# A mixture-of-experts encoder step on one core: later hand-overs while experts are gathered

## The reference

```python
h = rmsnorm(x, norm1_w) * (1.0 + sc1) + sh1
z = h @ w_in + b_in
ya = rglru(...)                       # 4 blocks of 128 channels
yb = mlstm(...)                       # 4 heads; state C, n carried over the tokens
x = x + g1 * (concat([ya, yb]) @ w_out)
h2 = rmsnorm(x, norm2_w) * (1.0 + sc2) + sh2
# peer, for each token, 8 heads:
q = rms(h2 @ wq)                      # 256 per head
v1, i1 = top_k(q1 @ k1.T, 16); v2, i2 = top_k(q2 @ k2.T, 16)
sv, si = top_k(v1 + v2, 16)           # of 256 candidates
expert = i1[si // 16] * 128 + i2[si % 16]
act = gelu(u[expert] . h2)
out = sum over 128 experts of softmax(sv) * act * v[expert]
y = rmsnorm(x + g2 * out, final_norm_w)
```

## Time and profile before

| | |
|---|---|
| median of 3 runs | 3409.78 us (3409.64 to 3411.5) |
| the profiled execution: its own time | 3413.67 us |
| its span, in which all rows stand | 3411.9 us |
| mean granted PE clock | 0.674 of full |
| busy PE, DVE, ACT, POOL | 70%, 65%, 58%, 36% of the span |
| DMA read and written | 1182.83 MB and 9.25 MB |
| first gather issued at | 531.31 us |

### The profile page before, as it was taken

One profiled execution on the slowest core, in us unless ns is written; L12 is line 12 of the kernel. 1 busy time (PEld: TensorE's weight loads), 2 busy tenths in 40 slices (PEclk: granted clock), 3 DMA queues, 4 the chain that ended last, 5 costly groups with the idle time before them and its releaser, 6 DMA issues.

```text
span 3411.9 us, 45621 instructions
## 1 busy us (share of the span) xinstructions
PE 2374.3 (70%) x15134; PEld 1117.1 (33%) x15134; DVE 2217.8 (65%) x5518; ACT 1985.6 (58%) x6404; POOL 1237.9 (36%) x1118
## 2 busy tenths in 40 slices
PE   7999976777567766666666666666666666676554
PEld 5665453333223322332322232223222332232110
DVE  5677255654576767666666666667666666667655
ACT  3332144554576766666576666666666666666655
POOL 0000102222344444444344434444444444434332
PEclk9999987888666666566556656666666566655555
DMA  7231317777999999999999999999999999999998
GB/s 276 85 113 60 78 69 248 279 281 268 364 420 401 369 421 420 397 420 420 417 393 420 420 404 413 420 420 394 420 420 420 395 420 420 420 393 420 421 421 349
DMA packets 184160, 1195.09 MB, mean 350 GB/s; under 512 B 22122, under 2 KB 32906, under 8 KB 44530
## 3 DMA queue, kind: packets, MB, share of 16 engines
q0 software_dynamic: 154240, 1113.16, 80.6%
q1 hardware_dynamic: 29684, 79.02, 6.7%
HBM read 1182.83 MB, written 9.25 MB: 349 GB/s over the span
## 4 chain that ended last, share of the span: by engine, by line
PE 36%; DMA 31%; ACT 18%; DVE 8%; issue 3%; POOL 3%; SPq 0%; DVEq 0%; POOLq 0%; ACTq 0%
DMA r_w<-in_peer_uv,gidx 11%; DMA r_vo<-in_peer_uv,gidx 10%; DMA r_yT<-in_peer_uv,gidx 9%; PE ps L953 9%; PE ps L1013 7%; PE ps L770 6%; PE ps L913 4%; PE ps L1002 4%; ACT mixc L1349 3%; PE ps L827 3%; ACT mixc L1348 3%; ACT r_qk L1353 3%; ACT L1348 2%; ACT mixc L1346 2%; DVE r_vo L1937 2%
## 5 line engine op out<-in xcount | busy, mean ns | idle before, releaser
L674 POOL DMA_INDIRECT r_vo<-in_peer_uv,gidx x272 | 321.2, 1181 | 509.1 <-PE ps L1013 465.1
L1013 PE MATMUL ps<-r_vo,r_qk 128*32 128x256 f32 x2176 | 264.9, 575 | 343.4 <-ACT r_qk L1353 342.8
L1345 ACT ACTIVATE mixc<-mixc 128x1 f32<-128x1 f32 x1056 | 208.8, 198 | 497.4 <-DVE r_yT L1937 153.4
L1013 PE MATMUL ps<-r_qk 128*32 128x256 f32 x2176 | 264.7, 575 | 284.4 <-ACT r_qk L1353 284.4
L674 POOL DMA_INDIRECT r_w<-in_peer_uv,gidx x241 | 286.8, 1190 | 458.2 <-PE ps L1013 442.0
L1349 ACT ACTIVATE mixc<-mixc 128x1 f32<-128x1 f32 x1056 | 409.1, 387 | 35.2
L674 POOL DMA_INDIRECT r_yT<-in_peer_uv,gidx x271 | 281.9, 1040 | 400.9 <-PE ps L1013 371.9
L674 POOL DMA_INDIRECT r_qk<-in_peer_uv,gidx x272 | 314.5, 1156 | 304.6 <-PE ps L1013 279.4
L1348 ACT ACTIVATE mixc<-mixc 128x1 f32<-128x1 f32 x1056 | 395.9, 375 | 1.0
L1013 PE MATMUL ps<-r_yT,r_qk 128*32 128x256 f32 x2168 | 254.4, 562 | 159.4 <-ACT r_qk L1353 145.6
L1353 ACT ACTIVATE r_qk<-prm,mixc 128x32 f32<-128x32 f32 x1056 | 340.0, 322 | 34.3
(11 more groups left out here) (331 smaller groups left out, 4380.0 us busy)
## 6 DMA issues: line engine op xcount, KB each, us to landing
r_w<-in_ada_w SPq DMA_DIRECT2D x18, 1024.0 KB, 5.4
r_w<-in_w_lin SPq DMA_DIRECT2D x16, 512.0 KB, 7.1
r_w<-in_peer_wq SPq DMA_DIRECT2D x6, 1024.0 KB, 21.0
r_hT<-in_peer_wq SPq DMA_DIRECT2D x6, 1024.0 KB, 13.2
r_vo<-in_peer_uv,gidx POOLq DMA_INDIRECT x272, 13.9
r_qk<-in_peer_uv,gidx POOLq DMA_INDIRECT x272, 14.9
r_yT<-in_peer_uv,gidx POOLq DMA_INDIRECT x271, 15.0
r_vo<-in_x_prompt SPq DMA_DIRECT2D x8, 512.0 KB, 7.1
```

The lines of the kernel that those rows point to most:

```text
L674: pool.indirect_dma_start(ring[i], None, table, bass.IndirectOffsetOnAxis(gidx_t[:, t % 2, h, c:c + 1], 0)).then_inc(e_ld[i], 16)
L1013: mm = nc.tensor.matmul(ps[c * DEC:(c + 1) * DEC, q // 2, (q % 2) * QC:(q % 2 + 1) * QC], diag[:, s % 4, :], row[:, D + c * QC:D + (c + 1) ...
L1345: wch.mark(nc.scalar.activation(sq[:, i:i + 1], d, ACT.Square, scale=GELU_C ** 0.5 / TANH_K))
```

## The change

Five things are changed; no computation is added or left out.

1. The chunk loop: from step 4 on `gated` and `turn_y` handle chunk i - 2 (`turned_y` i - 3), with `gated` ahead of `mixed_heads`. The work for tile 0 (x1 norm, scaling, turn, query, scores, route of head 0) moves one step earlier, and the norm of route 1 is moved ahead of the slot loop on ACT.
2. Hand-overs in the slot loop: a projection's pieces on PE go from offsets 0, 1, 5, 6 to 0, 2, 7, 9, its evictions on DVE from 3 and 8 to 7 and 14, `scaled` from 11 to 18; in a route the ACT part of the query goes from offset 0 to 2, the scores from 2 to 4, the first DVE step from 5 to 8, `copy_places` from 17 to 23 (12 to 18 in the short form).
3. The tables: projections every 14 slots in place of 10 (the last tile at slot 104 in place of 74), so `JOIN` goes from 92 to 108; routes 4 to 15 every 13 or 14 slots in place of gaps from 8 to 23.
4. Tile 1 takes its heads 4 to 7 first (`number`, `tile_head`, `SETS`), and POOL and ACT wait for one head's indices and gates at a time, not for those of a whole set.
5. The start of a tile: `final_sum` from slot 1 to 3, with what follows it; the sample head's query goes with the seventh head of a tile in place of the head S_AT = 5.

```diff
-JOIN = 92
+JOIN = 108
-SETS = [((0,), (1,), (2, 3), (4, 5), (6, 7)), ((0, 1), (2, 3), (4, 5, 6, 7))] + [
+SETS = [((0,), (1,), (2, 3), (4, 5), (6, 7)), ((4, 5), (6, 7), (0, 1, 2, 3))] + [
     ((0, 1, 2, 3), (4, 5, 6, 7))] * (NT - 3) + [((0,), (1,))]
-FAST = (1, 2, 3, 8, 9, 12, 13, 14, 15)
-ROUTE_AT = {1: -4, 2: 7, 3: 13, 4: 22, 5: 37, 6: 53, 7: 69, 8: 92, 9: 102, 10: 116, 11: 132,
-            12: 146, 13: 154, 14: 162, 15: 170, 16: 180}
-ROUTE_AT.update({m: 180 + 16 * (m - 16) for m in range(17, (NT - 1) * HEADS + S_STEPS)})
-PROJECT_AT = {t: 4 + 10 * (t - 1) for t in range(1, NT)}
+FAST = (1, 2, 3)
+ROUTE_AT = {1: -7, 2: 5, 3: 11, 4: 22, 5: 36, 6: 50, 7: 64, 8: 78, 9: 92, 10: 106, 11: 120,
+            12: 133, 13: 146, 14: 159, 15: 172}
+ROUTE_AT.update({m: 184 + 16 * (m - 16) for m in range(16, (NT - 1) * HEADS + S_STEPS)})
+PROJECT_AT = {t: 4 + 14 * (t - 1) for t in range(1, NT)}
+PROJECT_AT[NT - 1] = 104
@@ number, sample_head, slots
-            return t * HEADS + h
+            return t * HEADS + ((h + 4) % HEADS if t == 1 else h)
-            return t - 1 if t and h == S_AT else t if (t, h) == (NT - 2, S_AT + 1) else None
+            p = number(t, h) % HEADS
+            return t - 1 if t and p == HEADS - 2 else HEADS - 1 if (t, p) == (NT - 2, HEADS - 1) else None
-                            slots.append((t, h, q, c, len(builds) - 1, number(t, heads_of[-1])))
+                            slots.append((t, h, q, c, len(builds) - 1, number(t, h)))
-            return 10 if m in FAST else 15
+            return 13 if m in FAST else 18
@@ PE, slot loop
-                    elif u < NT - 1 and s - at in (0, 1, 5, 6):
-                        project(u, (s - at) // 5, range(4 * ((s - at) % 5), 4 * ((s - at) % 5) + 4))
+                    elif u < NT - 1 and s - at in (0, 2, 7, 9):
+                        k = 2 * ((s - at) % 7)
+                        project(u, (s - at) // 7, range(k, k + 4))
-                    if s - ROUTE_AT[m] == 2:
+                    if s - ROUTE_AT[m] == 4:
                         scores(*tile_head(m))
-                if t and j == 4:
+                if t and j == 6:
                     sum_squares(t - 1, 4)
@@ ACT, slot loop
-                    if s == at + (9 if u < NT - 1 else 4):
+                    if s == at + (15 if u < NT - 1 else 9):
                         x1_norm(u)
-                    if s == ROUTE_AT[m] and m < number(NT - 1, 0):
+                    if s == ROUTE_AT[m] + 2 and m < number(NT - 1, 0):
                         query(*tile_head(m))
@@ DVE, chunk loop
                 carry(i)
+                if i == 4:
+                    projected(0, 1)
+                if i >= 4:
+                    gated(i - 2)
                 if i >= 1:
                     mixed_heads(i - 1)
-                if i >= 1:
+                if i in (1, 2):
                     gated(i - 1)
@@ DVE, slot loop
-                    if s == at + 3:
+                    if s == at + (7 if u < NT - 1 else 8):
                         projected(u, 0)
-                    if s == at + (8 if u < NT - 1 else 3):
+                    if s == at + (14 if u < NT - 1 else 8):
                         projected(u, 1)
-                    if s == at + (11 if u < NT - 1 else 6):
+                    if s == at + (18 if u < NT - 1 else 12):
                         scaled(u)
-                if t and j == 1:
+                if t and j == 3:
                     final_sum(t - 1, 4)
...
```

More of the change, by code:

```diff
@@ L380, in routes, with build_at @@
         def routes(s):
[L382 to L386 removed]
+            return [m for m in range(1, N_ROUTES) if 0 <= s - ROUTE_AT[m] <= 26]
+        def build_at(s, wide):
+            b = first.index(s) if s in first[:-2] else None
+            return b + 1 if b is not None and (first[b + 1] - s > 4) == wide else None
         def tile_head(m):
[L390 removed]
+            t, p = m // HEADS, m % HEADS
+            return t, (p + 4) % HEADS if t == 1 else p
         def piece(m):
[L394 removed]
+            return 13 if m in FAST else 18
         x_rows = [A["x_prompt"][0, t * P:(t + 1) * P, :] for t in range(NT - 1)] + [A["x_sample"][0]]
@@ L1416, in _ @@
             query(0, 1)
+            norm(1)
             for s in range(N_SLOTS):
```

126 lines of the change are left out of this document (63 added, 63 removed).

## The result

The changed kernel takes 3331.75 us (median of 4 runs, 3328.37 to 3335.28) against 3410.25 us (3409.64 to 3411.5): ratio 0.9769, 95% interval 0.9753 to 0.9786, or 78.5 us less by the medians. Its profiled execution took 3333.69 us with a span of 3331.1, so 80.8 us less span than before's 3411.9. A second series with the same kernel gave 0.9764 (0.9749 to 0.9780). The forecast was 3322 us with a range of 3279 to 3372: right in sign and within the range, 10 us too low.

What follows compares the result with a forecast made beforehand. It took DVE and PE waiting for each other to hold the first tile, and the gathers to bound later slices. Terms of -10, -60, -4 and -14 summed to -88 us, predicting 3322 us, range 3279 to 3372.

Steps and rivals of the forecast that it cites:

- term 2: First tile: longer hand-overs win two thirds of PE's 90.6 us of waiting, -60 us, bounds 0 and -90.
- Term 1: Chunk loop: `gated` one step later saves 3.0 us a step, -10 us in all, bounds -15 and -3.
- `keys` and `carry` stand outside this, and so do PE's turns: Chunk loop: these lie outside the circle of 7.6 us, 8.1 with hand-overs, that remains in a step.
- The clock rival: First tile: every projection piece runs slow, so its gain is only 26 us; 3356 us, chance 0.18.
- The floor rival: First tile reaches the DMA's floor, gaining 90 us there; 3292 us, chance 0.20.
- The slower rival: First tile: projections on six places set the pace whatever the distances, 4.23 us a slot to 118; 3434 us, chance 0.07.
- Term 3: Tile 1: routes 13 slots apart, as close as 8 before, save 4 us, bounds 0 and -5.6.
- Fifteen slots are over 39 us, so I cost it at nothing: SP's queue into tile 1: loads ready from slot 116, needed from 131 and 133, cost nothing.
- Six places still cover a landing: First tile up to `JOIN` at 108: six places, 17 us, cover a landing of 7 to 15 us.
- Term 4: Later tiles: moving the long query saves 15 us, later `final_sum` costs 1; -14 us, bounds -17 and +15.
- just covered: Later tile starts: `mix` waits some 5 us more for `final_sum`, covered by four gathers, 10 us, under way.
- a new dip where `final_sum` stands: Tile starts: a sign that would show the prediction wrong; no window with a DMA share below 0.9 was expected.

Runs made afterwards that it cites:

- Run 5: Changed kernel with `gated` between `nd_done` and the write of `hh`, and ACT's tile 0 copies ahead of its squares and root: 3328.07 us.
- run 3: Changed kernel with the chunk loop of the kernel before, everything behind it as changed: 3335.32 us.
- run 7: Changed kernel with SP loading the final norm's rows and tile 0's x1 rows ahead of four query weights: 3327.58 us.
- run 8: Changed kernel with eight places from slot 112 in place of 108 (`JOIN`): 3328.05 us.
- Run 11: Changed kernel with the five steps of the final norm back at their old slots: 3342.21 us.
- run 1: Changed kernel with projection pieces, evictions and norm at the old distances, pitch and routes as changed: 3380.94 us.
- run 6: The changed kernel again, nothing edited, as a yardstick: 3330.89 us.

## Why the prediction was right, and where not

**The bound.** The reading that the first tile is held by DVE and PE waiting for each other at the eviction, and not by transfers, was right, and it carries the larger part of the result. Restoring the old distances gives back 49 of the 78.5 us, and 78.5 us of waits (544 to 851) at the line that I had named. It was not the whole: with DVE's wait back, the first tile was still 35 us shorter than before (421.2 against 456.2 from the first dot). In the prediction the wider pitch had no share of its own in term 2, and stood otherwise as a rival that makes the kernel slower. What it and the new routes win by themselves is known only as this remainder.

**Term 1, chunk loop, -10: measured -3.4** (by the loop's own steps -0.4 in three). Even the 3.4 is not shown to be a gain: the one profile before has its first dot at 547.62, and the eight with the changed loop lie between 543.54 and 548.27. The step that failed is "`keys` and `carry` stand outside this, and so do PE's turns". PE's order has tile 0's query and scores ahead of `turn_keys`, and they wait for ACT's copies behind the root; so the root was in the circle by another way. And `gated` ahead of `mixed_heads` put 1.5 us before `nd_done`, for which PE waits in `products` and `heads`. I had costed the added waits, but not what DVE's own work in a new place delays for PE. Run 5 cut both and took 4.3 us out of the same steps. The 11.1 us were no plain step either: at 477.45 DVE does two operations of tile 0's projection in it (L1811 and L1818, 0.69 us each), right ahead of the next `keys`. Without these 1.3 us the step is 9.8, and 1.7 us above the circle of 8.1, not 3.0. That the earlier first gather brings nothing of its own was right: run 3 has it 10.6 us later and the first dot at the same time.

**Term 2, first tile, -60: measured -69.2** for slots 0 to 128 (403.2 us, not 412), and -79.4 from the first dot, since the first gather came 13.5 us earlier and the dot only 3.4; bound -90. The windows over the two stretches, before and after, split it:
```profile
531.31:1003.77 472.46, 344.54 (x1932) 155.07 (x1932) 273.11 (x703) 256.16 (x787) 146.71 (x129) 0.75 0.86 318
```
```profile
517.76:921.00 403.24, 329.67 (x2006) 157.61 (x2005) 286.42 (x755) 266.56 (x817) 146.88 (x129) 0.82 0.93 365
```
PE's idle time fell from 127.9 to 73.6 us, by 54.3, close to the 60 that I had taken from its waits. The other 14.9 us are PE's own work, 344.54 down to 329.67 with no fewer instructions, at a granted clock of 0.82 and not 0.75. I had named that possibility in a rival ("better fed it also runs at the higher clock") and left it out of the sum. Part of the gain is a shift: 147.2 MB passed in place of 150.42. Over both tiles from the first dot the forecast was -64 and the result -79.4 + 9.2 = -70.2.

**The clock rival** (every piece slow, 3356 us) is out: 15 of the 28 pieces take 3.70 us, where it wanted none, and their sum is 121.9 us against 122.7 before. Its price was off too: "today half of each kind" is wrong, 17 of the 28 took 3.70 us before and the other 11 only 5.4 on average. By the same 2.44 us a piece that would have been 41 us and not 34. What the Trainium skill says (TensorE: Matmul & The Clock Gate, "HAM oscillation"), that work broken up by waits pays the warm-up anew for each stretch, fits the 13 pieces of 4.2 to 6.2 us and not the others, and over the stretch the granted clock rose. **The floor rival** (3292): the DMA share from 544 to 851 is 0.96 and PE is busy for 269.03 of those 307 us, so both are near full and the two dry spells at gather 109 and slot 128 keep the time above it. **The slower rival** needed 4.0 us a slot up to slot 118; the pace was 261.5 / 80 = 3.27 to slot 80 and (850.48 - 779.24) / 24 = 2.97 from there to 104, and gather 119 came at 887.69.

**Term 3, tile 1, -4: measured +9.2**, the wrong sign. Two steps failed, both of them costed at nothing. "Fifteen slots are over 39 us, so I cost it at nothing": the rows of the final norm and of x1 landed 4.3 and 7.5 us after they were needed. I had set the need against the time until slot 131, but not the time that 4 MB take in a queue whose engines are full. Issues from 890 to 960 (KB each, median us to landing):
```profile
r_hT<-in_peer_wq SPq DMA_DIRECT2D x2, 1024.0 KB, 21.6
r_w<-in_peer_wq SPq DMA_DIRECT2D x2, 1024.0 KB, 33.9
```
And the bytes themselves, 3.6 MB more on SP's queue in tile 1 than before, are 8.5 us of transfer moved from a tile that had room to one that hasn't (run 7). I had counted bytes for the floor of the first tile and not for the second.

**"Six places still cover a landing"** was right as put, and beside the point: what failed at `JOIN` was gather 109, which needs a place that PE's last projection frees at slot 104, four slots ahead, while POOL runs six ahead. It waited 15.34 us (run 8). I had looked at how long a landing takes and not at who had the new places before.

**Term 4, later tiles, -14: measured -6.7**, and not 2.5 us in each: tile 2 is 1.5 us shorter, tiles 3 to 6 by 0.0 to 0.5, and tile 7 by 4.0 (323.3 against 327.3), for which I have no cause. The periods are 327.1 to 327.9 up to tile 6, not near 326. The old dip, where the two queries met the end of the final norm, is gone as said. But `final_sum` two dots later was not "just covered": POOL waits 7.40 us and a window falls to a share of 0.67. This is one of the signs that the prediction gave for being wrong, a new dip where `final_sum` stands, and for this term it came true. Run 11 adds what the forecast had no term for: with that gone, the query dries the queue in its place. In such a tile stalls of 8 to 9 us each stand at the edge of the ring's cover, and removing one of them earns nothing while the next is there.

**The sum.** -88 against -80.8 in the spans is closer than its terms. From the first dot on the first tile brought 19 us more than forecast, and the three other terms together 27 us less. That these nearly cancel is luck.

## What to carry to other kernels

Where two engines stand in line for each other, lengthen the hand-over before cutting any work: 49 us came from moving a projection's evictions and scaling by four to seven slots and its pieces two slots apart. When a stage becomes bound by transfers, its bytes turn from free to costly, so recount in which tile each load falls and what queues behind it. Before you cost a wait at nothing, follow the late item through every in-order queue that it passes, the engine's own new order among them.

## What the runs showed of the hardware

A full share is no full rate. In tile 3 of the changed kernel, 65 us behind gather 385, a window at a share of 1.02 moves some 370 GB/s, where gathers alone move 420 (from 1720 to 1740, 8.38 MB at a share of 100.9%, which is 415 GB/s at a full share). The window, and the queues from 1655 to 1675 (packets, MB, share of 16 engines):
```profile
1657.00:1672.00 15.00, 7.96 (x55) 4.09 (x52) 8.00 (x25) 7.35 (x26) 6.08 (x6) 0.53 1.02 370
```
```profile
q0 software_dynamic: 953, 6.91, 90.4%
q1 hardware_dynamic: 771, 0.68, 11.2%
```
SP's transfers (packets of 0.9 KB on average) take 11.2% of the engines for 9% of the bytes, which is little. But the gathers' own 6.91 MB take 90.4% of 20 us, 382 GB/s at a full share against 415: their packets take longer too while the small ones run. Why was not tried.

PE's work is not a fixed number of microseconds. From the first dot to gather 129, 1938 instructions took 328.6 us at a granted clock of 0.77 (run 1) and 310.7 at 0.85 (run 6). The kernel with fewer waits had the shorter work too; that the one follows from the other was not tested by itself.

The same instructions ran through the chunk loop at different times: `keys(8)` started between 506.30 and 510.30 us in the eight profiles with an unedited loop. Effects of 3 us in the whole can't be read off one profile by absolute times; differences between two events inside it are steadier.
